# Two-layer decoder trunk in fp32: results of experts 0 to 6 go through DRAM rows in place of scatter products, and the last norm is split by tile and half

## What is computed

```python
def moe_swiglu(h, w_router, w_gate, w_up, w_down):
    logits = (h @ w_router).astype(jnp.float32)
    top_v, top_i = lax.top_k(logits, TOP_K)
    top_w = jax.nn.softmax(top_v, axis=-1)
    gates = jnp.sum(jax.nn.one_hot(top_i, N_EXPERTS, dtype=jnp.float32) * top_w[..., None], axis=-2)
    y = jnp.zeros_like(h)
    for e in range(N_EXPERTS):
        y = y + gates[..., e:e + 1] * swiglu(h, w_gate[e], w_up[e], w_down[e])
    return y
...
            x = x + moe_swiglu(rmsnorm(x, od_norm_ffn[i]), od_w_router[i], od_w_gate[i],
                               od_w_up[i], od_w_down[i])
    return rmsnorm(x, final_norm)
```

## Time and profile before

| what | value |
|---|---|
| device time, median of 3 runs | 1489.27 us (1486.58 to 1491.92) |
| profiled execution: device time | 1491.28 us |
| its span, first to last instruction | 1488.8 us |
| PE busy | 1445.4 us (97%) |
| DVE busy | 1132.1 us (76%) |
| ACT busy | 938.1 us (63%) |
| POOL busy | 33.6 us (2%) |
| mean DMA rate over the span | 292 GB/s |
| mean granted PE clock | 0.985 of full speed |

### The profile page before, as it was taken

How to read it: one execution, slowest core, us unless ns; L and a number is a source line. 1 busy time by engine, 2 the same in 40 slices (tenths; PEclk the granted TensorE clock), 3 DMA queues, 4 the chain that set the end, 5 groups by cost and what they waited for, 6 DMA issues and landing times.

```text
span 1488.8 us, 16959 instructions
## 1 busy us (share of the span) xinstructions
PE 1445.4 (97%) x7037; PEld 1213.4 (82%) x7037; DVE 1132.1 (76%) x850; ACT 938.1 (63%) x731; POOL 33.6 (2%) x37
## 2 busy tenths in 40 slices
PE   9987999999999999999999999999999999999996
PEld 8975788888987888888888888888888888888885
DVE  4674645544454888998989898898899899889885
ACT  3553544334443777777777777777777777777773
POOL 0000000000001000000000000000000000000000
PEclk9987999999999999999999999999999999999998
DMA  9642455564543599999999999999999999999991
GB/s 312 188 142 62 151 197 170 183 209 145 186 141 114 186 388 377 358 359 391 347 375 369 374 361 354 389 362 363 387 350 368 379 361 365 372 370 366 357 375 72
DMA packets 135106, 434.42 MB, mean 292 GB/s; under 512 B 11273, under 2 KB 28657, under 8 KB 119281
## 3 DMA queue, kind: packets, MB, share of 16 engines
q1 hardware_dynamic: 130544, 424.24, 78.3%
q0 software_dynamic: 2016, 7.35, 1.4%
q10 hardware_dynamic: 2464, 1.69, 0.4%
HBM read 431.15 MB, written 2.11 MB: 291 GB/s over the span
## 4 chain that ended last, share of the span: by engine, by line
PE 91%; DVE 5%; ACT 2%; issue 1%; DMA 0%; SPq 0%; POOL 0%; DVEq 0%; POOLq 0%; ACTq 0%
PE ps L1645 28%; PE ps L1647 28%; PE ps L1646 28%; PE ps L2164 2%; DVE lo L1059 1%; PE ps L1829 1%; ACT hi L686 1%; PE ps L2109 0%; PE ps L1707 0%; PE ps L2110 0%; DMA raw<-in_ev_w_in_dram 0%; DVE work L1102 0%; PE ps L2083 0%; PE ps L1935 0%; PE ps L1811 0%
## 5 line engine op out<-in xcount | busy, mean ns | idle before, releaser
L1059 DVE TENSOR_TENSOR lo<-raw,hi 128x2048 fp32r<-128x2048 f32 (+1 forms) x403 | 903.3, 2283 | 105.9 <-ACT hi L686 104.4
L686 ACT ACTIVATE hi<-raw 128x2048 fp32r<-128x2048 f32 (+1 forms) x403 | 770.8, 1916 | 259.7 <-PE ps L1647 254.8
L1645 PE MATMUL ps<-hi,xT_hi 128*128 128x512 f32 (+2 forms) x1216 | 474.4, 390 | 3.3 <-DVE lo L1059 1.6
L1647 PE MATMUL ps<-hi,xT_lo 128*128 128x512 f32 (+2 forms) x1216 | 468.3, 385 | 0.0
L1646 PE MATMUL ps<-lo,xT_hi 128*128 128x512 f32 (+2 forms) x1216 | 468.3, 385 | 0.0
L1645 PEld LDWEIGHTS ps<-hi,xT_hi 128*128 128x128 f32 x1216 | 229.1, 188 | 50.0 <-issue 2.7
L1647 PEld LDWEIGHTS ps<-hi,xT_lo 128*128 128x128 f32 x1216 | 228.6, 188 | 46.9
L1646 PEld LDWEIGHTS ps<-lo,xT_hi 128*128 128x128 f32 x1216 | 228.9, 188 | 43.8
L1645 PE MATMUL ps<-hi,hT_hi 128*128 128x512 f32 x536 | 210.2, 392 | 0.9 <-DVE hT_lo L1359 0.9
L1647 PE MATMUL ps<-hi,hT_lo 128*128 128x512 f32 x536 | 208.8, 390 | 0.0
L1646 PE MATMUL ps<-lo,hT_hi 128*128 128x512 f32 x536 | 208.6, 389 | 0.0
(11 more groups left out here) (252 smaller groups left out, 786.4 us busy)
## 6 DMA issues: line engine op xcount, KB each, us to landing
raw<-in_od_w_gate_dram SPq DMA_DIRECT2D x112, 1024.0 KB, 7.7
raw<-in_od_w_up_dram SPq DMA_DIRECT2D x112, 1024.0 KB, 7.8
raw<-in_od_w_down_dram SPq DMA_DIRECT2D x112, 1024.0 KB, 7.4
raw<-in_od_w_qkv_dram SPq DMA_DIRECT2D x12, 1024.0 KB, 5.3
raw<-in_ev_w_gate_dram SPq DMA_DIRECT2D x11, 1024.0 KB, 5.2
raw<-in_ev_w_up_dram SPq DMA_DIRECT2D x11, 1024.0 KB, 5.2
raw<-in_ev_w_down_dram SPq DMA_DIRECT2D x11, 1024.0 KB, 5.1
raw<-in_ev_w_in_dram SPq DMA_DIRECT2D x4, 1024.0 KB, 11.1
```

What stands on the lines that cost most here:

```text
L686: act.activation(unit(hi, n), unit(raw, n), ACT.Copy).then_inc(hi_ready, 1)
L1059: dve.tensor_tensor(unit(lo, n), unit(raw, n), unit(hi, n).bitcast(F32), ALU.subtract)\
L1645: pe.matmul(out, s_hi, m_hi, start=start, stop=False, skip_group_check=True)
L1647: return pe.matmul(out, s_lo, m_hi, start=False, stop=stop, skip_group_check=True)
```

## The change

The results of experts 0 to 6 are no longer scattered by products. ACT copies a result in float32 to y_out (`y_copy`), POOL stores it to DRAM (result_d, 128 rows for each expert). In expert 1, DVE works out for each token the two rows of result_d at which its results are and their gates (`slot_numbers`). In expert 7, behind its store of the seventh result, POOL fetches four tiles of 128 rows by indirect DMA (two token tiles, the higher and the other of two slots), and DVE adds them to x, times the gates, between the splits of units 24 to 28 (`add_result`). place is transposed only in expert 7. Expert 7's own result is still scattered by products; its last unit makes all products of the first half of the columns first, and the copies to y_hi and y_lo go by half. keep_busy there is gone. The last norm stands inside both branches, begins with tile 1, and tile 0 is scaled and stored in two halves.

```diff
-            for t in range(T):
-                sp.wait_ge(out_ready, t + 1)
-                sp.dma_start(out_d[0, P * t:P * t + P, :], work[:, t, :]).then_inc(out_stored, 16)
-            sp.wait_ge(out_stored, 16 * T)
+            for i, (t, first, n) in enumerate(STORES):
+                sp.wait_ge(out_ready, i + 1)
+                sp.dma_start(out_d[0, P * t:P * t + P, first:first + n], work[:, t, first:first + n])\
+                    .then_inc(out_stored, 16)
+            sp.wait_ge(out_stored, 16 * len(STORES))
...
+                    pool.wait_ge(y_copied, e)
+                    pool.dma_start(result_d[P * (e - 1):P * e, :], y_out).then_inc(y_stored, 16)
+                pool.wait_ge(slots_ready, 1)
+                pool.wait_ge(y_stored, 16 * (NE - 1))
+                for i in range(2 * T):
+                    pool.indirect_dma_start(result_row(i), None, result_d, bass.IndirectOffsetOnAxis(
+                        ap=rslot_id[:, i // 2, i % 2:i % 2 + 1], axis=0)).then_inc(results_landed[i], 16)
...
-            def y_high(e):
+            def y_copy(e):
 
                 act.wait_ge(units_used, first_of(e + 1))
-                act.activation(y_hi, ps[:, 0:2, :].rearrange("p a n -> p (a n)"), ACT.Copy).then_inc(y_hi_ready, 1)
+                if e:
+                    act.wait_ge(y_stored, 16 * e)
+                act.activation(y_out, ps[:, 0:2, :].rearrange("p a n -> p (a n)"), ACT.Copy).then_inc(y_copied, 1)
...
+            def last_norm_std(added):
+
+                act.wait_ge(*added)
+                act.activation(work[:, 1, :], x[:, 1, :], ACT.Square, accum_out=stat[:, 1:2]).then_inc(squares_done, 1)
+                for n, (t, _, _) in enumerate(STORES[0:T]):
+                    act.wait_ge(var_ready, VARS[4] + n)
+                    act.activation(stat[:, 2 + t:3 + t], stat[:, t:t + 1], ACT.Sqrt).then_inc(std_ready, 1)
...
-                    act.wait_ge(placeT_done, e + 1)
-                    act.activation(placeT[:], ps[:, 6, 0:SEQ], ACT.Copy).then_inc(placeT_ready, 1)
+                    if e == NE - 1:
+                        act.wait_ge(placeT_done, 1)
+                        act.activation(placeT[:], ps[:, 6, 0:SEQ], ACT.Copy).then_inc(placeT_ready, 1)
...
-                y_high(NE - 1)
-                act.wait_ge(scatter_added, 4 * NE - 2)
+                act.activation(root[:], root[:], ACT.Sqrt)
+                act.wait_ge(y_half_done, 1)
+                act.wait_ge(y_stored, 16 * (NE - 1))
+                act.activation(y_hi[:, 0:W], ps[:, 0, :], ACT.Copy).then_inc(y_hi_ready, 1)
+                act.wait_ge(units_used, U_END)
+                act.activation(y_hi[:, W:D], ps[:, 1, :], ACT.Copy).then_inc(y_hi_ready, 1)
+                last_norm_std((scatter_added, 2))
...
+
+            def slot_numbers():
+
+                val, last = rslot[:, :, 0:NE - 1], NE - 1
+                for e in range(last):
+                    ins = dve.tensor_scalar(rslot[:, :, e], rplace[:, :, e], float(P * e + 1), None, ALU.add)
+                link(ins)
+                link(dve.tensor_tensor(val, val, rpick[:, :, 0:last], ALU.mult))
+                link(dve.tensor_reduce(rslot_at[:, :, 0], val, AX.X, ALU.max))
+                link(dve.tensor_reduce(rslot_at[:, :, 1], val, AX.X, ALU.add))
+                link(dve.tensor_tensor(rslot_at[:, :, 1], rslot_at[:, :, 1], rslot_at[:, :, 0], ALU.subtract))
+                for t in range(T):
+                    for m in range(2):
+                        link(dve.scalar_tensor_tensor(out=rsel[:, t, 0:last], in0=rslot[:, t, 0:last],
+                                                      scalar=rslot_at[:, t, m:m + 1], in1=rgate[:, t, 0:last],
+                                                      op0=ALU.is_equal, op1=ALU.mult))
+                        link(dve.tensor_reduce(rslot_gate[:, t, m:m + 1], rsel[:, t, 0:last], AX.X, ALU.add))
+                link(dve.tensor_scalar(rslot_at[:], rslot_at[:], -1.0, 0.0, ALU.add, ALU.max))
+                dve.tensor_copy(rslot_id[:], rslot_at[:]).then_inc(slots_ready, 1)
...
+            def add_result(i):
+
+                t, m = i // 2, i % 2
+                dve.wait_ge(results_landed[i], 16)
+                link(dve.scalar_tensor_tensor(out=x[:, t, :], in0=result_row(i), scalar=rslot_gate[:, t, m:m + 1],
+                                              in1=x[:, t, :], op0=ALU.mult, op1=ALU.add))
...
+            def last_norm():
+
+                dve.wait_ge(squares_done, 5)
+                mean_square(4, 1)
+                link(dve.tensor_tensor_reduce(work[:, 0, :], x[:, 0, :], x[:, 0, :], 1.0, 0.0, ALU.mult, ALU.add,
+                                              stat[:, 0:1]))
+                mean_square(4, 0)
+                dve.wait_ge(gain_loaded[4], 16)
+                for t, first, n in STORES:
+                    if first == 0:
+                        dve.wait_ge(std_ready, VARS[4] + 1 - t)
+                        link(dve.reciprocal(stat[:, 2 + t:3 + t], stat[:, 2 + t:3 + t]))
+                    part = slice(first, first + n)
+                    dve.scalar_tensor_tensor(out=work[:, t, part], in0=x[:, t, part], scalar=stat[:, 2 + t:3 + t],
+                                             in1=gain[:, 0, part], op0=ALU.mult, op1=ALU.mult).then_inc(out_ready, 1)
...
 
                     if e:
                         used(0)
-                        y_low(e - 1)
                     used(GATE_AT[1])
                     multiply(e, 0)
-                    if e:
-                        add_scattered(0, e - 1)
                     used(GATE_AT[1] + 2)
                     g_hT_low(e, 0)
-                    if e:
-                        add_scattered(1, e - 1)
                     used(UP_AT[1])
-                    if e:
-                        add_scattered(2, e - 1)
-                    used(UP_AT[1] + 2)
-                    if e:
-                        add_scattered(3, e - 1)
+                    if e == 1:
+                        slot_numbers()
                     used(DOWN_AT[0])
                     multiply(e, 1)
                     used(GATE_AT[2])
                     if e + 1 < NE:
-                        dve.wait_ge(placeT_done, e + 1)
                         make_place(e + 1)
...
                     used(DOWN_AT[1])
                     multiply(e, 2)
+                    if e == NE - 1:
+                        for i in range(2 * T):
+                            used(DOWN_AT[1] + i + 1)
+                            add_result(i)
...
-                y_low(NE - 1)
+                for m in range(2):
+                    half = slice(W * m, W * m + W)
+                    dve.wait_ge(y_hi_ready, 1 + m)
+                    dve.tensor_tensor(y_lo[:, half], ps[:, m, :], y_hi[:, half].bitcast(F32), ALU.subtract)\
+                        .then_inc(y_ready, 1)
                 for i in range(4):
                     add_scattered(i, NE - 1)
-                dve.wait_ge(scatter_added, 4 * NE)
+                dve.wait_ge(scatter_added, 4)
+                last_norm()
...
+                if i < 2:
+                    pe.wait_ge(y_ready, i + 1)
                 if i == 0:
-                    pe.wait_ge(y_ready, e + 1)
-                    pe.wait_ge(placeT_ready, e + 1)
-                elif e < NE - 1:
-                    pe.wait_ge(scatter_added, 4 * e + i)
+                    pe.wait_ge(placeT_ready, 1)
...
-                    for jj in range(2):
+                    final = n == U_END - 1
+                    for jj, m in ((0, 0), (1, 0), (0, 1), (1, 1)) if final else ((0, 0), (0, 1), (1, 0), (1, 1)):
                         j = 2 * (q % 2) + jj
...
+                        if final and (jj, m) == (1, 0):
+                            ins.then_inc(y_half_done, 1)
                     ins.then_inc(units_used, 1)
...
-                if e:
-                    pe.wait_ge(scatter_added, 4 * e)
+                pe.wait_ge(place_ready, e + 1)
...
                     up(e, 0, 0, 1)
-                    if e:
-                        scatter(0, e - 1)
                     gate(e, 1, 0, 1)
                     g_transpose_h(e, 0, 0)
+                    gate(e, 1, 2, 3)
+                    up(e, 1, 0, 1)
+                    up(e, 1, 2, 3)
                     if e:
-                        scatter(1, e - 1)
-                    gate(e, 1, 2, 3)
-                    if e:
-                        scatter(2, e - 1)
-                    up(e, 1, 0, 1)
-                    if e:
-                        scatter(3, e - 1)
-                    up(e, 1, 2, 3)
+                        pe.wait_ge(y_copied, e)
                     down(e, 0, 0, 1)
-                    transpose_place(e)
+                    if e == NE - 1:
+                        transpose_place(e)
...
                     down(e, 3, 0, 1, 2, 3)
-                keep_busy(9, 6)
                 for i in range(4):
                     scatter(i, NE - 1)
```

62 lines of the change are left out of this document (27 added, 35 removed).

## The result

The changed kernel takes **1472.35 us** (median of 4 executions, 1470.55 to 1474.29), the kernel before 1488.66 us beside it (1486.58 to 1491.92). The ratio is 0.9889, with a 95% interval of 0.9866 to 0.9911: 16.3 us less, and beyond the scatter. The forecast was 1473.0 us.

A forecast was written before the change was run, and what follows sets the result against it. PE was taken as the bound, with DVE and the ring of raw buffers close behind. -15.2 + 0.8 + 1.2 + 1.5 - 4.6 = -16.3 us gave a median of 1473.0 us, range 1467.5 to 1478.5 for 8 in 10.

The forecast's parts named there:

- Products and transposes: Scatter pairs and place transposes taken from PE in seven experts, all on the path: -15.2 us.
- Slot numbers: In expert 1, a 3.5 us lump on DVE between units 9 and 10 makes PE wait: +0.8 us.
- Adds in the last expert: DVE's four adds of fetched results between splits make PE wait for units 27 and 28: +1.2 us (0 to 2.0).
- The burst of DMAs: Store and fetches in the last expert delay the weights beyond the cover: +1.5 us (0 to 4.6).
- The tail: After the last down product, the end comes 12.1 us behind it against 16.7 before: -4.6 us.
- the later one counts: In the tail, the end follows the later of 11.7 us (behind the stores) and 12.0 us (branch behind the norm).
- The sum: All terms for the whole kernel together: -16.3 us, a median of 1473.0 us.
- (b): The covers suffice everywhere, no stall at all: -19.8 us, 1469.5 us; chance 0.17.
- (d): DMAs become the bound in all of experts 1 to 6: 1509.6 us; chance 0.04.
- (a): Last expert's burst costs 4.6 instead of 1.5 us, DVE's stalls 1.6 more: 1477.7 us; chance 0.14.
- (c): In the tail, the branch's stall returns in full or other slowness loses its 3.1 us: 1476.1 us; chance 0.10.

The follow-up runs named there:

- Run 1: Changed kernel with two idle products that nothing reads in the place of each of the 28 scatter pairs: 1483.78 us, ratio 0.9967.
- run 2: Changed kernel with slot_numbers made in two parts, each in front of a wait DVE has anyway in expert 1: 1470.62 us, ratio 0.9879.
- run 3: Changed kernel with the four adds of fetched rows moved in front of DVE's waits for transposed halves in the last expert: 1470.9 us, ratio 0.9879.
- run 8: Changed kernel with four more 512 KB stores to a spare tensor queued behind the four fetches in the last expert: 1474.45 us, ratio 0.9904.
- 5: Changed kernel with the edits of run 2 and run 3 together: 1469.9 us, ratio 0.9869.
- run 9: The kernel of run 5 with tile 0 of the last norm scaled and stored in one piece: 1468.59 us, ratio 0.9859.

## Why the prediction was right, step by step

- **Products and transposes, -15.2 us: right.** Expert 2 to 6 take 119.13 us where they took 121.33, 2.20 each; forecast were 119.0 for the period and 15.2 / 7 = 2.17 for each expert. Run 1 measured the pairs alone at 0.48 us (forecast 0.49). The waits that were added, PE's for y_copied and ACT's for the store, show no time in any view.
- **Slot numbers, +0.8 us: right.** The lump was 3.52 us (3.5), the stall 0.92 us, by run 2.
- **Adds in the last expert, +1.2 us: right, slightly high.** 1.32 us for an add (1.31), a stall of 1.0 us by run 3.
- **The burst of DMAs, +1.5 us: mis-sized.** It cost PE nothing. The range (0 to 4.6) held it. The mechanism was as told: the ring ran empty, weights landed after 11.6 us in the middle, and ACT waited 5.4 us. But the value was taken above the low end, by giving weight to the 3.4 us of the largest landings. The low end, the burst's bytes at 414 GB/s less what is regained, was the one to trust, and run 8 fits that rate, as one point can. The Trainium skill's rule of turns between queues ("DMA: Bandwidth & Descriptors", Queues, rings and completion order) made it about 4 us of delay inside the cover. The trace agrees that the cover holds, and with the even shares in part. From 1355 to 1359 us the queue of the weights (q1) and that of the fetches (q0) have about half each (packets, MB, share of the DMA engines):

```profile
q1 hardware_dynamic: 209, 0.86, 53.2%
q0 software_dynamic: 207, 0.78, 49.0%
```

  In the 4 us before and behind, q0 has 36.6 and 36.5%: while the fetches land, the weights keep more than half.
- **The tail, -4.6 us: the span's part was mis-sized, -3.3 us.** The first store was issued 7.2 us behind the last down product (7.3) and the last scaling ended at 8.7 (8.8). What failed is the step behind it, "the later one counts: 12.1" (8.8 + 3.15 is 11.95 besides). Both of its terms were wrong. The branch does not wait for the last scaling: it is taken 7.3 us behind the last down product and over at 10.9, not 12.0, so that it is the earlier one. The end behind the stores was put at 2.9 us behind the last scaling and is 4.0 (1465.8 to 1469.8), since SP's wait is 3.3 us instead of 2.4; and on top DVE's last instruction is 0.7 us late (0.7 to 0.9 in runs 1, 3 and 8 as well, but level in 2, 5 and 9): 13.4 us. That the third store or the smaller ones lengthen it is ruled out by run 9, at 3.1 us with two whole ones; what does is open. 1.1 us were saved outside the span, which the prediction did not consider, so that the time lost with the tail fell by 4.4 us after all.
- **The sum.** Forecast -16.3, measured -16.3 in the medians, -17.0 at equal clock and -17.5 by the pieces. The mechanism of the largest term, PE's time, was right. That the medians meet the forecast to 0.1 us is luck: the errors of the burst (-1.5), the tail (+1.3) and the time outside (-1.1) leave 1.3 us, and the clock and the scatter of the medians took back the rest.
- **Rivals.** (b), no stall at all, is true of the burst only: the other two stalls cost 0.92 and 1.0 us. (d), the DMAs as the bound, fell at once: 379 GB/s in a whole expert with PE busy all the time. (a), the worse burst, is what run 8 looks like with twice the bytes. (c), the stall behind the branch coming back, fits in its size for about half: 1.6 of its 3.1 us are lost at the end (0.9 in the landing, 0.7 in DVE's end). But no run shows that the branch causes them, and its stall itself is over before.

## What to carry to other kernels

Products taken from a PE that never waits were worth their start-to-start time here, and small products of its own can be replaced by DMAs that go through DRAM, if the queues have the bytes to spare at the rate seen in the trace and the burst fits the ring and the lead behind it. The work that replaces them belongs in front of waits that its engine has anyway, not between the splits that feed PE: the same instructions cost 1.9 us in one place and nothing in the other. Before a difference of 1 or 2 us between medians is believed, compare the granted clock of the executions or the pieces of the profiles.
